# One fused decoder-trunk kernel: extra token tiles interleaved, one-hots made a turn ahead, first condition round in chunks

## What is computed

```python
mod = silu(c) @ ada_w + ada_b                  # [2048] @ [2048, 12288]
sh1, sc1, g1, sh2, sc2, g2 = split(mod, 6)
xm = x * (1 + sc1) + sh1
q, k, v, z, gate_logits = split(xm @ w_in)     # 2048 -> 9216
y_att = dilated_mixture(q, k, v, rel_bias)     # 8 heads, 3 patterns
y_sgu = spatial_gating(z)
mix = (sigmoid(gates) * [y_att @ wb0, y_sgu @ wb1]).sum() @ w_out
x = layer_norm(2**0.25 * x + g1 * mix)
hm = x * (1 + sc2) + sh2
# 16 experts in 4 groups; the best group of a token, its top 2 experts:
for e in range(16):
    y += combine[:, e] * ((silu(hm @ w_gate[e]) * (hm @ w_up[e])) @ w_down[e])
x = layer_norm(2**0.25 * x + g2 * y)
```

## Time and profile before

| | us |
|---|---|
| median of 3 runs (1968.63 to 1972.21) | 1969.88 |
| profiled execution, own time | 1971.56 |
| its span | 1969.0 |
| PE busy (8790 products) | 1764.0 |
| PE weight loads busy | 954.9 |
| DVE busy | 508.3 |
| ACT busy | 163.1 |
| moved by DMA | 629.83 MB, 320 GB/s over the span |

### The profile page before, as it was taken

How to read it: one execution, slowest core, us unless ns; L and a number is a source line. 1 busy time by engine, 2 the same in 40 slices (tenths; PEclk the granted TensorE clock), 3 DMA queues, 4 the chain that set the end, 5 groups by cost and what they waited for, 6 DMA issues and landing times.

```text
span 1969.0 us, 21226 instructions
## 1 busy us (share of the span) xinstructions
PE 1764.0 (90%) x8790; PEld 954.9 (48%) x8791; DVE 508.3 (26%) x938; ACT 163.1 (8%) x340; POOL 2.5 (0%) x9
## 2 busy tenths in 40 slices
PE   5897999999999999968999888998889888899984
PEld 2345888688888874453433233332243222432321
DVE  0532526656355001230121120211111111111114
ACT  0000013200000000040000011000020000200000
POOL 0000000000000000000000000000000000000000
PEclk8998999999999999988999999999999999899997
DMA  9888775678667633323689995899989999599995
GB/s 394 353 335 275 328 288 225 256 306 342 271 275 322 256 158 129 161 87 145 253 343 428 428 427 240 354 427 429 427 354 428 428 427 429 230 370 389 428 428 221
DMA packets 49177, 629.83 MB, mean 320 GB/s; under 512 B 5615, under 2 KB 8080, under 8 KB 10152
## 3 DMA queue, kind: packets, MB, share of 16 engines
q1 hardware_dynamic: 47512, 621.58, 76.2%
q10 hardware_dynamic: 1552, 6.57, 0.8%
HBM read 624.46 MB, written 3.67 MB: 319 GB/s over the span
## 4 chain that ended last, share of the span: by engine, by line
PE 67%; DMA 24%; DVE 5%; SPq 2%; issue 2%; ACT 1%; DVEq 0%; ACTq 0%
PE bank L765 37%; PE bank L567 18%; DMA ring<-in_w_down 11%; PE bank L578 8%; DMA ring<-in_w_up_gate 8%; DMA ring<-in_ada_w 3%; PE bank L590 2%; DMA ring<-in_w_in 1%; DVE ada_rows L1310 1%; SPq L411 1%; DVE region_a L1601 1%; PE bank L635 1%; PE bank L585 1%; PE bank L798 0%; DVE region_a L1269 0%
## 5 line engine op out<-in xcount | busy, mean ns | idle before, releaser
L567 PE MATMUL bank<-ring,region_b 128*64 128x512 f32 x2048 | 461.4, 596 | 44.9 <-DMA ring<-in_w_up_gate 30.6
L765 PE MATMUL bank<-region_a,ring 128*128 128x256 f32 x1792 | 393.0, 381 | 13.4 <-DMA ring<-in_w_in 13.4
L765 PEld LDWEIGHTS bank<-region_a,ring 128*128 128x128 f32 x1792 | 341.4, 191 | 63.6 <-DMA ring<-in_w_in 13.8
L567 PEld LDWEIGHTS bank<-ring,region_b 128*64 128x64 f32 x2048 | 141.6, 137 | 338.1 <-issue 281.6
L578 PE MATMUL bank<-ring,region_f 128*64 128x512 f32 (+1 forms) x1536 | 260.3, 525 | 43.3 <-DMA ring<-in_w_down 38.4
L1310 DVE SCALAR_TENSOR_TENSOR ada_rows<-ring,condT,ada_rows 128x512 f32<-128x512 f32 x293 | 220.2, 752 | 10.1
L578 PEld LDWEIGHTS bank<-ring,region_f 128*64 128x64 f32 (+1 forms) x1536 | 87.1, 128 | 202.0 <-issue 137.5
L1601 DVE TENSOR_TENSOR region_a<-bank,region_a 128x512 f32<-128x512 f32 x128 | 79.5, 683 | 212.9 <-PE bank L590 211.9
L765 PE MATMUL bank<-ring,region_a 128*128 128x512 f32 x256 | 119.9, 626 | 6.0 <-DVE region_a L1287 6.0
L765 PE MATMUL bank<-ring,region_b 128*128 128x512 f32 x256 | 110.3, 592 | 1.3 <-issue 1.3
L1606 DVE TENSOR_TENSOR sgu_wT<-bank,g2x 128x512 f32<-128x512 f32 x32 | 22.1, 691 | 242.9 <-PE bank L578 242.9
(11 more groups left out here) (165 smaller groups left out, 688.6 us busy)
## 6 DMA issues: line engine op xcount, KB each, us to landing
ring<-in_w_up_gate SPq DMA_DIRECT2D x128, 2048.0 KB, 20.6
ring<-in_w_down SPq DMA_DIRECT2D x64, 2048.0 KB, 21.8
ring<-in_ada_w SPq DMA_DIRECT2D x48, 2048.0 KB, 13.1
ring<-in_w_in SPq DMA_DIRECT2D x34, 2048.0 KB, 17.5
ring<-in_w_branch SPq DMA_DIRECT2D x8, 2048.0 KB, 17.7
ring<-in_w_out SPq DMA_DIRECT2D x8, 2048.0 KB, 11.6
ring<-in_w_in SPq DMA_DIRECT2D x4, 1024.0 KB, 4.8
region_a<-in_x_T ACTq DMA_DIRECT2D x4, 512.0 KB, 26.3
```

Of the source, the lines that this page charges most:

```text
L567: last = nc.tensor.matmul(bank_of(x, j)[n * c:n * c + n, 0:2 * m], tokens(x, 8 * half + k), w[:, k, :, m * c:m * c + m], start=(half == 0 ...
L765: return nc.tensor.matmul(out, lhsT, rhs, start=start, stop=stop)
```

## The change

Four things are done.

1. **Start.** The first pair of condition units (scale and shift of the first 512 channels) is laid out by chunks of 128 channels and loaded, multiplied, summed and taken chunk by chunk; the first round's row unit and `x` come in matching parts, and PE multiplies one chunk's rows while the next chunk's condition is loading. Both condition units of the pair are multiplied by PE.
2. **Rounds.** Row units 1 and 3 get buffers of their own (`region_b`, `region_d`) instead of a ring slot, so a row unit waits for the round two before. DVE takes unit 2r+2 between the halves of unit 2r+3. The small loads are spread over four places of the stream, each behind a later unit.
3. **Extra tiles.** For an expert with one or two extra tiles the steps of the first section (gather, turn, products) stand between parts of the first tile's products, and the two scatters of sections E and F behind the next half of the first tile's down product. Both halves of the first unit are released together, behind the last extra tile's products.
4. **Turns.** DVE makes `hot` of the next turn at the middle of a turn (before its third expert). Its last turn is therefore a copy behind the loop.

The core of the diff:

```diff
+ODD_ROWS = (AT["rows", 1], AT["rows", 3])
@@ row_parts
+            odd = n in ODD_ROWS
+            v_part = region_b[:, :] if odd else slot(n)[:, 0:8 * UW]
+            z_part = region_d[:, :] if odd else slot(n)[:, 8 * UW:12 * UW]
@@ SP
+            def first_condition(c):
+                cols = slice(c * KC * P, (c + 1) * KC * P)
+                for m in (SC1, SH1):
+                    sp.dma_start(slot(AT["ada", ADA_UNITS.index((m, 0))])[:, cols], ada_w_d[m * 4][:, cols])\
+                      .then_inc(first_ada[c], 16)
+            def first_row(c):
+                for dst, kind, width in zip(row_parts(AT["rows", 0]), ("v", "z"), (2, 1)):
+                    first, cols = IN_COL[kind] // UW, slice(c * UW, (c + 1) * UW)
+                    sp.dma_start(dst[:, :, cols], w_in_d[first:first + width, :, cols].rearrange("u p n -> p u n"))\
+                      .then_inc(first_rows[c], 16)
+            after_unit = {BY_ROWS + 1: store_bias_rows, BY_ROWS + 2: load_gating, BY_ROWS + 3: load_bias,
+                          BY_ROWS + 4: load_router}
+            first_condition(0)
+            first_condition(1)
+            first_row(0)
+            first_condition(2)
+            first_row(1)
+            first_condition(3)
+            first_row(2)
+            x_part(1)
+            sp.wait_ge(first_mm, 2)
+            load_unit_half(RING, 0)
+            load_unit_half(RING + 1, 0)
+            first_row(3)
+            sp.wait_ge(ada_mm, 2)
+            load_unit_half(RING, 1)
+            load_unit_half(RING + 1, 1)
-                        if i > 0:
-                            sp.wait_ge(rows_used, 2 * (i - 1) + part + 1)
+                        if i >= 2:
+                            sp.wait_ge(rows_used, 2 * (i - 2) + part + 1)
-                if (kind, i) == ("w", BY_ROWS):
-                    small_loads()
+                if kind == "w" and i in after_unit:
+                    after_unit[i]()
@@ PE, front
+            def first_multiply(c):          # 32 products of 128 x 128: both units' chunk c
+            def first_step(c):              # 2 sums
+            def first_rows_part(c, jobs):   # the products of chunk c's slice of xmT
+            first_multiply(0)
             mm(psum[5][0:H, 0:TOE], rel[:, :], buckets, True, True).then_inc(s_toep, 1)
+            first_step(0)
+            first_multiply(1)
+            for c in range(3):
+                pe.wait_ge(first_rows[c], 32)
+                pe.wait_ge(xm_ready, c + 1)
+                first_rows_part(c, row_jobs)
+                first_step(c + 1)
+                if c < 2:
+                    first_multiply(c + 2)
+            first_rows_part(3, row_jobs[:4]).then_inc(rows_used, 1)
+            ada_multiply(2)
+            first_rows_part(3, row_jobs[4:5])
+            ada_step(2)
+            first_rows_part(3, row_jobs[5:]).then_inc(rows_used, 1)
+            ada_step(3)
-            for r in range(4):
+            for r in range(1, 4):
@@ DVE, front
-                    ada_part(a + 1, range(KC))
-                ada_take(a)
+                    ada_part(a + 1, range(8))
+                    ada_take(a)
+                    ada_part(a + 1, range(8, KC))
+                else:
+                    ada_take(a)
@@ PE, experts, section A
-            extras("A")
-            pe.wait_ge(y_ready, ne * 2 + 1)
-            gate_up(0, 0, 0, first).then_inc(half_used, 1)
+            if len(xs) == 1:
+                extra("gather")(1)
+                pe.wait_ge(y_ready, ne * 2 + 1)
+                gate_up(0, 0, 0, range(4))
+                extra("turn")(1)
+                gate_up(0, 0, 0, range(4, 8))
+                extra("A")(1)
+            elif len(xs) == 2:
+                extra("gather")(1)
+                pe.wait_ge(y_ready, ne * 2 + 1)
+                gate_up(0, 0, 0, range(3))
+                extra("turn")(1)
+                gate_up(0, 0, 0, range(3, 6))
+                extra("gather")(2)
+                extra("A")(1)
+                extra("turn")(2)
+                gate_up(0, 0, 0, range(6, 8))
+                extra("A")(2)
@@ extra("A"), behind gate_up(x, 0, 0)
+                        if x == xs[-1]:
+                            last.then_inc(half_used, 2)
@@ PE, experts, sections E and F (F alike)
-            extras("E")
+            for x in xs:
+                extra("E")(x)
             down(0, 0, first).then_inc(half_used, 1)
+            if 0 < len(xs) < 3:
+                extra("add E")(1)
             turn(hid[1]).then_inc(t_full, 1)
             down(0, 0, last).then_inc(y_full, 1)
+            if len(xs) == 2:
+                extra("add E")(2)
@@ DVE, experts
+            def mark_tokens(g, first):      # the hot loop of before
+                    if more and le == GRP // 2:
+                        mark_tokens(g, GRP)
+            mark_tokens(0, 0)
+            with nc.Fori(0, NE // GRP - 1, engines=[mybir.EngineType.DVE], hint_back_edge=True) as g:
+                rest = turn_of_experts(g, True)
+            rest_last = turn_of_experts(NE // GRP - 1, False)
```

More of the change, by code:

```diff
@@ L81, with fills @@
 NFRONT = len(STREAM)
+ODD_ROWS = (AT["rows", 1], AT["rows", 3])
+def fills(n):
+    return n // RING - sum(m <= n and m % RING == n % RING for m in ODD_ROWS)
 NW = len(W_UNITS)
@@ new lines, in _ @@
+            x_part(1)
[6 more added lines that the diff above has]
+            load_unit_half(RING + 1, 1)
+            for n, (kind, i) in list(enumerate(STREAM))[RING + 2:]:
+                if kind != "rows":
+                    unit_used(sp, n - RING)
+                if kind == "rows":
+                    for part, (dst, kind, width) in enumerate(zip(row_parts(n), ("v", "z"), (2, 1))):
+                        if i >= 2:
+                            sp.wait_ge(rows_used, 2 * (i - 2) + part + 1)
+                        landed = odd_rows[part] if n in ODD_ROWS else loaded[n % RING][part]
+                        first = IN_COL[kind] // UW
+                        rows = w_in_d[first:first + width, :, i * 4 * UW:(i + 1) * 4 * UW]
+                        sp.dma_start(dst, rows.rearrange("u p kn -> p u kn")).then_inc(landed, 16)
+                    continue
+                if kind == "ada" and ADA_UNITS[i][0] == SC1:
+                    x_part(ADA_UNITS[i][1])
+                for h in range(2):
+                    load_unit_half(n, h)
+                if kind == "w" and i in after_unit:
+                    after_unit[i]()
@@ L625, in d, with gather @@
                         return ne * dve_count(x, "all") + dve_count(x, event)
-                    if sec == "A":
+                    def gather(q):
+                        for a in range(TT):
+                            for c in range(C):
+                                col = c * (D // C) + q * 512
+                                last = nc.tensor.matmul(own[n * c:n * c + n, :], hotx[:, a, 0:n],
+                                                        x1[:, a, col:col + 512], start=(a == 0), stop=(a == TT - 1),
+                                                        tile_position=(0, n * c), skip_group_check=True)
+                        last.then_inc(xp, 1)
+                    if sec == "gather":
                         pe.wait_ge(xd, ne * dve_count(x, "all") + 1)
+                        gather(0)
+                    elif sec == "turn":
                         for q in range(R):
@@ L1670, in _ @@
                 scaled(acc, ln2g, ln2b, a, TT, out_ready)
[L1671 to L1672 removed]
+            rest()
+            rest_last()
 _OUT = (1, T, D)
```

231 lines of the change are left out of this document (159 added, 72 removed).

## The result

| | before | after |
|---|---|---|
| median, us (4 runs each) | 1969.91 (1968.63 to 1972.21) | 1938.68 (1935.69 to 1941.14) |
| profiled execution, span | 1969.0 | 1934.0 |

The changed kernel takes 0.9828 of the time, 95% interval 0.9807 to 0.9848: 31.2 us less by the medians, 35.0 by the spans of the profiled executions (the one after was the fastest of its four, 1935.69). The forecast was a gain of 50.9 us and a time of 1920.7. The measured time lies 18 us above it, inside the wide range of 1905 to 1944 and outside the narrower one of the likeliest case, 1914 to 1926.

A forecast was written before the change was run, and what follows sets the result against it. The prediction held the front bound by PE's waits and the experts by the DMA's. Gains 3.8 + 16.0 + 10.0 + 12.9 + 4.0 + 4.2 = 50.9 us off 1971.56 gave 1920.7, range 1905 to 1944.

The forecast's parts named there:

- the likeliest case: Whole kernel: the prediction's own forecast of 1920.7 us, range 1914 to 1926, chance 0.48.
- the fourth rival: Experts: interleaving gives little, as code, waits or a fetch replace the old gaps; 1939, or 1925 for one DVE fetch; chance 0.16.
- The start: Front, up to round 1: round 1 starts at 61.6 instead of 67.66, a gain of 6.1 us.
- The rounds: Front rounds: DVE's new order makes each 32.0 us, two rounds 64.0 against 61.7, a loss of 2.3 us.
- Rival 2: Front rounds: DVE does not bind them, 27.3 us per round, kernel 1911 us; chance 0.12.
- The small loads: Second product unit: spreading the loads removes the stall behind the bias rows' store, gaining 16.0 us with 6.6 to spare.
- Rival 3: Third product unit: the store still delays the next pair and PE stops at 203.6; 1929 at 8 us of stop; chance 0.14.
- Rival 1: Start: the new row chunks move as slowly as the store, start 52 us later, kernel 1973 us; chance 0.04.
- Sections A, E and F: Experts with extra tiles: interleaving gains 10.0 us in turn 0, 4.0 in turn 1 and 4.2 in turn 3.
- The turns: Starts of three turns: with one-hots made early, PE's gather starts 4.3 us sooner each, 12.9 us in all.
- The stop on issue: Head of the last turn: DVE, leaving its loop for a copy, may stop 4.5 us on a fetch; 1925 if unhidden.
- rival 5: Mixed sections A to F of three experts: PE runs at 1.2 GHz, 250 us more, 2171 us; chance 0.02.

The follow-up runs named there:

- a2: Kernel after, but SP issues the fourth row chunk of round 0 ahead of the first halves of condition units 2 and 3: 1937.26 us.
- a1: Kernel after, but DVE makes all 16 multiply-adds of unit 2r+3 and only then takes unit 2r+2, as before the change: 1927.96 us.
- b3: Kernel after, but the small loads stand all together behind the first product unit and the bias behind the second, as before: 1940.4 us.
- a3: Kernel after, but DVE makes the next turn's one-hots at the end of a turn, as before: 1957.02 us.
- 144 increments: a1 plus 144 increments of an unread semaphore ahead of PE's first wait, which only move PE's later code: 1939.22 us.
- 32 to 144 increments: Six kernels, a1 plus 32, 64, 96, 112, 128 or 144 unread semaphore increments that move PE's later code: 1918.82 to 1944.68 us.

## Why the prediction was right and wrong, step by step

**Which side, and the range: right.** Of the sum of 50.9, 35.0 came. That the time lies inside the range is in part luck: some 25 us of terms came out worse and 9 better, by causes worked out below. The likeliest case did not hold. The time is that of the fourth rival (1939), a fetch that takes back the gain; but that is only one of the two causes, the start is the other, and the interleaving itself did not give little.

**The start: wrong.** The step that failed is "from its end to the round's first product": the sum started DVE's second half at the landing, 53.3. It starts at the taking, 59.73, which waits for PE's sum of unit 2 (58.59), and that sum is late because the fourth row chunk landed late (6.88 us) and its eight products ran in 6.48 us at the lower clock; 8 such products take 3.67 in a2. But the chunk is not the root: with it early, a2 has the sum at 57.04 all the same, since PE then waits for unit 2's second half. The landing was also late by itself: in a1 the wait of 5.88 us ends at 57.32, 4.0 behind the forecast. The windows move 350 x 25 + 421 x 25 + 419 x 7.3 = 22.3 MB by then, where 21.3 had been counted: 1.0 MB more, and the first window moves 350 GB/s and not 371. What the 1.0 MB is isn't shown; the issue of row unit 1 stands right behind, at 35.99. Round 1 at 68.70 is 7.1 later than forecast: 4.0 by the landing, 2.3 by the taking, the rest by the last steps (57.32 to 66.44 in a1 in 9.1 us where 8.3 were counted; its last sum takes 1.84 us behind a wait of 4.76, and 1.02 at round 3).

**The rounds: right.** 32.0 us were forecast and 32.8 and 32.3 measured, by the cause named, the taking between the halves. Rival 2 (1911) is out for the change, and a1 shows that it is what the old order gives: 29.3 and 27.5 us.

**The small loads: right in size.** 15.4 against 16.0. The store runs at 51 GB/s with a share of 0.46 (53 and 0.48 before), from about 154 to 183 and not from 147 to 177. PE never waits there, so how much of the margin of 6.6 us was left can't be read. Rival 3 (1929) is out. What failed is the place of the cause: the sum gives all 16.0 to the spreading, and b3 has it without. Rival 1 (1973) is out: the share is 1.02 from 25 to 50, where the new row chunks land. The Trainium skill, "DMA: Bandwidth & Descriptors", section "Why a DMA increments its semaphore by 16 and not by 1", says that a copy from SP's queue uses the largest number of engines up to 16 that divides its slowest dimension on both sides. That is 8 for the store of 8 heads and 16 for a chunk over 128 partitions; the trace agrees, 0.46 in the store and 1.02 with the chunks.

**Sections A, E and F: right but for section A of turn 1.** In turn 0 section A runs from 874.64 to 893.74 + 10.57/3 = 897.3, 22.6 us, where 23.9 were forecast. Before it took 30.3. E and F take from 941.4 to 976.7, 35.3 against 38.4: 3.1 gained of 3.6. Together they gain 10.8, where 10.0 were forecast. E and F of turns 1 and 3 gain 1.1 us each, for 0.8 and 0.9 (by the prediction's own terms the 0.9 should read 1.1). Section A of turn 3 takes 17.4 us without its stop of 4.63, for 20.9: the 3.3 forecast came. In turn 1 it takes 17.8 without its stop of 3.34, for 18.4: of 3.2 only 0.6 came. There the gather of the extra tile's tokens, with the stop inside it, has 4.67 us of products (1.05 + 3.62), and 1.92 before.

**The turns: the size was low.** 4.3 per turn, 12.9 in all, were forecast; a3 shows 18.3, since the gather also runs at full clock (3 x 14.08 against 16.20, 15.74 and 17.00 before). The 16.20 stood in the rows; the sum did not take it.

**The stop on issue: foreseen on DVE, costly on PE.** The prediction weighed a fetch on DVE at the head of the last turn, and 4.5 us if nothing hides it. The timeline of DVE after shows one where the last turn enters its variant with extra tiles, and it is hidden under the gather, which runs from 1648.56 to 1662.6:

```profile
1656.98 0.24 DVE L1760 TENSOR_SCALAR region_e<-slots,small 128x32 f32<-128x32 f32 x1 [5.10 <-issue]
```

In the kernel before, DVE has none at this step of the last turn, but one of 5.34 us at the same step of turn 1 (1175.95). So the row fits a taken branch; that leaving the loop for a copy adds a stop isn't shown. What failed is that the sum gave PE's stops no change: they are 26.5 - 10.6 = 15.9 us more. This is the larger of the two causes of the miss; the start with the rounds is 8.2, the stall 0.6. The faster gathers give 6.7 us back (48.94 of before less 42.22), and a rest of about 2 us, also better than forecast, lies within the single terms.

**The clock (rival 5): out.** The granted clock over the span was 0.974, and no stretch is as slow as this rival asks: the windows of sections A and E with F in turn 0 have 0.95 (876.0 to 909.8) and 1.00 (940 to 978).

## What to carry to other kernels

Whoever changes the code of an engine with branches and a loop moves all that lies behind it. Here that alone is worth up to 25.9 us, 1.3%, more than any single edit taken back in this study (7.6 to 18.3). So look at the time less the stops on issue beside the time itself, and try a few shifts before an edit is thrown away or praised. The difference of the two is an estimate: a stop can also slow the products behind it, and the sum moves by some microseconds without a shift. When a dependent chain is cut so that a result comes earlier, ask what the second part now waits for: here 10.5 us. Two parts of a change that remove the same stall are worth it once; take one out at a time to see.

## What the runs showed of the hardware

PE's stops on issue depend on where its code lies, with the same work: up to 9.27 us each (with 144 increments, at 976.17), 20.2 to 39.5 us in sum, and a shift of 16 instructions, from 128 to 144, is enough. In the kernel after, one of the two instruction queues, q8, landed 18 packets in turn 0 with its variant (853 to 1142), and one in turn 2, which has none (1408 to 1643). Its rows of the DMA view over the two stretches, packets, MB, share:

```profile
q8 instruction: 18, 0.29, 0.4%
...
q8 instruction: 1, 0.02, 0.0%
```

The count of a whole turn does not follow the stops, though: the kernel before and those with 32 to 144 increments have 8 or 9 packets in turn 2, also where PE has no stop there. The packets within the stops tell more. The 14 traces have 78 stops of over 1 us on PE behind 840. In each of the 58 that last 2.9 us or more at least one packet of q8 lands within the stop, two in each of the three of over 9 us; in none of the 20 that last 2.7 us or less does one land. So the long stops go together with instructions being loaded at that moment. That the load is what ends them, and whose instructions they are, the traces do not say.

The Trainium skill, "Runtime: NRT & Kernel Launch", section "Instruction fetch mechanics", says that code comes in blocks of 16 KiB and that a taken branch out of what is loaded must wait for a fetch. The size agrees on q8 (0.29 MB in 18 packets). That the stop can be 9 us, and that it can also come inside straight code some microseconds behind the branch (1168.27, within one gather of 16 products), these runs add. Which address starts a stop remains open: seven layouts do not give a rule.
